# A mixer whose transposes are woven into its tiles, with the two S5 shuffles on the GpSimd queue

## The chip, the cores and the metric

The kernel runs on one core of a Trainium2 chip. The metric is the device time of one execution in microseconds (us). The kernel before takes 2861.14 us, the median of three runs (2859.89 to 2865.21).

## The reference, cut to what matters

The kernel computes one layer of a decoder trunk for 2048 tokens of width 1024: a norm, a token mixer, a residual, a norm, a mixture of experts, a residual, a final norm. The mixer's four branches read one projection of the normalised input (14 blocks of 128 columns):

```python
proj = xn @ w_in                      # (2048, 1024) @ (1024, 1792)
ya = short_conv_mixer(a_b, a_c, a_x, conv_a_w)
yb = pool_mixer(p_u, pool_w, pool_b, pool_scale)
yc = s5_mixer(s_u, ...)               # complex diagonal state space, gelu, then a gated linear unit
yd = rglru_mixer(l_x, l_g, ...)
ys = jnp.stack([ya, yb, yc, yd], axis=2)
branch = jnp.einsum('bskw,kwd->bskd', ys, branch_w)
gates = jax.nn.sigmoid(xn @ merge_gate_w + merge_gate_b).reshape(bn, s, N_BRANCH, d)
merged = jnp.sum(gates * branch, axis=2)
return merged @ w_out
```

## The kernel before, in words

**Stages.** `mix_branches` does the norm, the projection and the four branches, `merge_branches` the gates, the merge, the output projection, the residual, the second norm and the router's logits. `route`, the experts and the last sum follow, and nothing of them changes. Between stages all engines meet at a barrier. Every product in fp32 is made of three matmuls: an operand is split into a rounded high part and the low rest, and high·high, low·high and high·low are added in PSUM.

**The mixer's loop.** The tokens go in four chunks (c = 0 to 3) of 512. In a chunk, ScalarE squares and sums the rows (`squares`), VectorE makes the reciprocal root (`rms_scale`), ScalarE scales the rows (`scale_rows`, L456). TensorE then transposes them to feature-major in 8 steps of 4 transposes into two alternating PSUM banks (`turn_x`, L641); for each step ScalarE writes the high part (`x_highs`, L463) and VectorE the low part (`x_lows`, L793), and only then is the bank free again. 14 projection tiles follow (`tile`, L632), each 24 matmuls of 128x512, in the order of `F_ORDER`. Between the tiles stand the small products: `gates(c)` (L649), `states_in` (L663, reads `u4`), `states_out` (L674 and L676, the S5 output of the chunk), `pool_out` (L655) and `glu(c)` (L686, reads `yn`). Each tile's bank comes from one of two rings of two banks: `gr` is emptied by ScalarE, `dr` by VectorE; a ring's order of use is a list (`g_turns`, `d_turns`), so a bank that is late stops what stands behind it in TensorE's program.

**The weights.** In chunk 0 the 14 weight tiles come raw from DRAM (`load_raw`, four buffers), ScalarE makes the high part (L445), GpSimd the low part (L419), and SyncE spills both to DRAM (`spill`); three buffers hold them for TensorE. In the later chunks SyncE reloads them tile by tile (`load_win`, L313), two or three tiles ahead.

**The S5 shuffles.** The S5 branch needs its input with time folded onto the partitions. `turn_u(c)` stores `su` to DRAM (L328, 512 KB) and, once that has landed, loads `u4` in another shape (L333, 4 DMAs of 128 KB). `turn_y(c)` does the same with the branch's output: one store of `yg4` (L339) and 8 loads into `yn` (L344, 64 KB each), after which `glu(c)` can run. Both are in SyncE's own in-order program: where SyncE waits for a store to land, the weight reloads behind it wait too. In chunks 2 and 3 `turn_y(c-1)` stands after the reload of tile 3, behind the store of the transposed input `xT` (L322, 4 MB) and the load of the next chunk's rows (L317, 2 MB), and `turn_u(c)` after the reload of tile 5. `glu(c-1)` and then `states_in(c, ...)` stand between tiles 3 and 4 on TensorE.

**GpSimd** does the 14 low parts in chunk 0 and then the cosine and sine tables (L429 to L434), and nothing in the rest of the mixer.

**The merge.** `merge_branches` takes the tokens in four trips of 512. A trip reads the transposed input (as high and low part) and the four branches' outputs from DRAM, and for each of 8 output tiles and 4 branches k makes a gate product (8 accumulation steps) and a branch product (2 steps), three matmuls a step (L1377). Weights go through a ring of four raw buffers; ScalarE and VectorE split them (L1312, L1446). Before the first trip SyncE issues in this order: weights of k=0, `xT` high and low (4 DMAs, 4 MB), two pieces of the branches, weights of k=1 to 3, six small parameters (L1243), `w_out`.

## Time and profile before

| | us |
|---|---|
| median of 3 runs | 2861.14 |
| the profiled execution | 2863.44 |
| its span | 2861.8 |
| TensorE busy in it | 2445.9 (85%) |
| VectorE, ScalarE, GpSimd busy | 1446.1, 1035.9, 531.4 |

TensorE is the busiest engine. The page's row of 40 slices shows where it isn't busy (a digit is the busy share of 71.5 us in tenths): the first eight slices are the mixer, the ninth holds the start of the merge.

```
PE   5788697949999999999999999279999999998930
DVE  6578373624343343343433433846546564655648
PEclk 9889798979998999999999999589999999999975
```

The chain of the page's fourth part is followed back from the last instruction and ends within the last stage, so it says nothing about the mixer. For the mixer the table of windows, the waits of a stretch and the timeline are read instead.

### The profile page before, as it was taken

How to read it: one execution, taken by the hardware profiler on the slowest of the kernel's cores; microseconds unless marked ns; L12 is line 12 of the kernel's file. 1: busy time of each engine (PE TensorE's matmuls, PEld its weight loads, DVE VectorE, ACT ScalarE, POOL GpSimd, SP SyncE). 2: the span in 40 equal slices, each digit the busy share in tenths (PEclk: the TensorE clock that was granted, in tenths of full speed). 3: DMA queues.
4: the chain of work that ended last, by engine and by line, in shares of the span. 5: the costliest groups of instructions: out<-in, count | busy, mean ns of one | idle time of the engine just before them, and what ended most of it. 6: DMA issues, size and time to landing. Idle time of an engine off the chain costs nothing. (4 is left out here: it accounts for less than half of the span.)

```text
span 2861.8 us, 36672 instructions
## 1 busy us (share of the span) xinstructions
PE 2445.9 (85%) x11820; PEld 1877.7 (66%) x11821; DVE 1446.1 (51%) x2190; ACT 1035.9 (36%) x1254; POOL 531.4 (19%) x380
## 2 busy tenths in 40 slices
PE   5788697949999999999999999279999999998930
PEld 4566575638866887588758884167677676777730
DVE  6578373624343343343433433846546564655648
ACT  3424132212221222122212221146556565666621
POOL 2500000000000000000000000424433443354451
PEclk9889798979998999999999999589999999999975
DMA  8653655484462446344544444258677767778766
GB/s 250 219 210 118 211 179 177 147 261 143 138 205 89 137 127 203 107 120 144 167 143 120 135 132 166 95 221 319 240 267 286 279 261 263 290 296 322 289 260 280
DMA packets 394811, 573.81 MB, mean 201 GB/s; under 512 B 34960, under 2 KB 226704, under 8 KB 394768
## 3 DMA queue, kind: packets, MB, share of 16 engines
q1 hardware_dynamic: 361152, 475.47, 48.4%
q0 software_dynamic: 21680, 76.57, 7.1%
q10 hardware_dynamic: 11936, 21.24, 2.0%
q8 instruction: 21, 0.34, 0.0%
q14 instruction: 22, 0.18, 0.0%
HBM read 449.73 MB, written 123.47 MB: 200 GB/s over the span
## 5 line engine op out<-in xcount | busy, mean ns | idle before, releaser
L1377 PE MATMUL mrgps<-act_hi,w_hi 128*128 128x512 f32 x1280 | 504.4, 394 | 37.0 <-DMA act_lo<-xn_feature_major 21.0
L1377 PE MATMUL mrgps<-act_lo,w_hi 128*128 128x512 f32 x1280 | 502.7, 393 | 0.0
L1377 PE MATMUL mrgps<-act_hi,w_lo 128*128 128x512 f32 x1280 | 502.1, 392 | 0.0
L1733 POOL TENSOR_TENSOR w_lo<-w_raw,w_hi 128x1024 fp32r<-128x1024 f32 x128 | 326.9, 2588 | 241.4 <-ACT w_hi L1724 241.4
L1728 DVE TENSOR_TENSOR w_lo<-w_raw,w_hi 128x2048 fp32r<-128x2048 f32 x124 | 302.6, 2482 | 35.4 <-ACT w_hi L1719 35.4
L1377 PEld LDWEIGHTS mrgps<-act_hi,w_hi 128*128 128x128 f32 x1280 | 243.5, 190 | 90.2 <-DMA act_lo<-xn_feature_major 22.3
L1377 PEld LDWEIGHTS mrgps<-act_hi,w_lo 128*128 128x128 f32 x1280 | 243.2, 190 | 51.2
L1377 PEld LDWEIGHTS mrgps<-act_lo,w_hi 128*128 128x128 f32 x1280 | 243.6, 190 | 50.3
L1446 DVE TENSOR_TENSOR w_lo<-w_raw,w_hi 128x1280 fp32r<-128x1280 f32 x129 | 192.5, 1492 | 132.4 <-ACT w_hi L1312 130.7
L1329 ACT ACTIVATE gt<-mrgps,mb 128x512 f32<-128x512 f32 x128 | 88.4, 690 | 446.8 <-PE mrgps L1377 446.8
L1861 PE MATMUL exps<-w_hi,xT_hi 128*128 128x256 f32 (+1 forms) x768 | 247.5, 322 | 1.9 <-DVE xT_lo L2053 1.9
L1861 PE MATMUL exps<-w_lo,xT_hi 128*128 128x256 f32 (+1 forms) x768 | 245.6, 320 | 0.0
L1861 PE MATMUL exps<-w_hi,xT_lo 128*128 128x256 f32 (+1 forms) x768 | 245.6, 320 | 0.0
L1312 ACT ACTIVATE w_hi<-w_raw 128x1280 fp32r<-128x1280 f32 x129 | 164.5, 1275 | 210.1 <-DVE tmp L1467 135.3
L1719 ACT ACTIVATE w_hi<-w_raw 128x2048 fp32r<-128x2048 f32 x128 | 237.9, 1906 | 5.7 <-DMA w_raw<-in_expert_w_dram 5.7
L1293 POOL DMA_DIRECT2D expert_rows<-zeros x32 | 29.8, 932 | 1081.9 <-DVE w_lo L1446 1028.5
L1397 PE MATMUL mrgps<-wout,merged 128*128 128x512 f32 x512 | 222.1, 593 | 6.7 <-DVE merged L1469 6.7
L1467 DVE SCALAR_TENSOR_TENSOR tmp<-gt,mrgps 128x512 f32<-128x512 f32 x96 | 66.1, 688 | 301.2 <-PE mrgps L1377 301.2
L632 PE MATMUL mixps<-mix_xT_hi,win_hi 128*128 128x512 f32 x448 | 185.0, 413 | 36.5 <-DVEq L866 16.9
L632 PE MATMUL mixps<-mix_xT_lo,win_hi 128*128 128x512 f32 x448 | 182.1, 406 | 0.0
L632 PE MATMUL mixps<-mix_xT_hi,win_lo 128*128 128x512 f32 x448 | 181.3, 405 | 0.0
L1397 PEld LDWEIGHTS mrgps<-wout,merged 128*128 128x128 f32 x512 | 96.3, 190 | 125.1 <-issue 116.7
(377 smaller groups left out, 3649.3 us busy)
## 6 DMA issues: line engine op xcount, KB each, us to landing
w_raw<-in_expert_w_dram SPq DMA_DIRECT2D x128, 1024.0 KB, 8.9
w_raw<-in_merge_gate_w_dram SPq DMA_DIRECT2D x132, 512.0 KB, 4.1
w_raw<-in_expert_w_dram SPq DMA_DIRECT2D x32, 2048.0 KB, 14.2
expert_rows<-zeros POOLq DMA_DIRECT2D x32, 1008.0 KB, 7.2
win_hi<-w_in_parts SPq DMA_DIRECT2D x42, 512.0 KB, 3.5
win_lo<-w_in_parts SPq DMA_DIRECT2D x42, 512.0 KB, 5.3
w_raw<-in_branch_w_dram SPq DMA_DIRECT2D x132, 128.0 KB, 3.9
expert_rows<-ysb ACTq DMA_DIRECT2D x64, 256.0 KB, 3.1
```

The costliest lines, as they stand in the source:

```text
L632: last = pe.matmul(bank[:], w[:, n % NW, cols], x[:, k], start=(k + j == 0), stop=(k == KD - 1 and j == 2))
L1293: pool.dma_start(dram["y"][ds(i * FILL, FILL), :].rearrange("(p r) (q n) -> p (r q) n", r=2, n=256), zeros[:].unsqueeze(1).to_broadcast([F ...
L1312: act.activation(w_hi[:, k % 2].rearrange("p k n -> p (k n)"), w_raw[:, k].rearrange("p k n -> p (k n)"), ACT.Copy).then_inc(w_hi_set, 1)
L1329: act.activation(gt[:], gbank[k % 2][:], ACT.Tanh, scale=0.5, bias=mb[:, k, ds(d, 1)]).then_inc(g_free, 1)
L1377: last = pe.matmul(bank[:], w[:, k % 2, kk], x[:, a], start=(kk == w_tiles[0] and x is act_hi and w is w_hi), stop=(kk == w_tiles[-1] and ...
L1397: last = pe.matmul(bbank[h][:], merged[:, kk, t * P:(t + 1) * P], wout[:, kk, h * 512:(h + 1) * 512], start=(kk == 0), stop=(kk == KD - 1))
L1446: dve.tensor_tensor(lo, w_raw[:, k].rearrange("p k n -> p (k n)"), hi.bitcast(F32), ALU.subtract).then_inc(w_split, 1)
L1467: dve.scalar_tensor_tensor(tmp[:], gt[:], 1.0, bbank[k % 2][:], ALU.add, ALU.mult).then_inc(b_free, 1)
L1719: act.activation(self.hi13[:, i], self.raw13[:, i], ACT.Copy).then_inc(self.high13, 1)
L1728: eng.tensor_tensor(self.lo13[:, i], self.raw13[:, i], self.hi13[:, i].bitcast(F32), ALU.subtract).then_inc(self.split13, 1)
L1733: eng.tensor_tensor(self.lo2[:, f], self.raw2[:, f], self.hi2[:, f].bitcast(F32), ALU.subtract).then_inc(self.split2, 1)
L1861: last = pe.matmul(bank[:, 0:n], x[:, k], weights[:, 2 * w + k // 4, cols], start=(k + i == 0), stop=(k == KD - 1 and i == 2))
```

## The change

1. `turn_u` and `turn_y` are issued by GpSimd. `turn_u(0)` stands after its eighth weight split, all others after the tables, in the order u(1), y(0), u(2), y(1), u(3), y(2), y(3). SyncE's program no longer holds a wait for them. The large transfers of a chunk stand after the reload of tile 4 (in chunk 0 after the spills of tiles 7 and 9, where they were after that of tile 1).
2. `first_tiles(c)` weaves the transposes with tiles 0 and 1.
3. The small products move: `gates(0)` before tile 8, `states_out(c-1)` ahead of all transposes, `glu(c-1)` behind tile 7 (that of chunk 0 behind tile 13 of chunk 1), `states_out(3)` behind tile 8 of chunk 3 in two banks of their own. ScalarE's and VectorE's parts of the S5 output are cut up between the eight steps of `x_highs` and `x_lows`.
4. The raw merge weights are loaded during chunk 3 into a buffer which they share with `xin`. `x_hi` and `x_lo` of chunk 3 stay in SBUF, and the merge takes chunk 3 first (the trips go 3, 0, 1, 2), so its start loads neither. Its pieces are issued first, then the parameters.

```diff
+    LAG = 4
-                return f(*range(10)) + gates(0) + f(10, 11)
+                return f(*range(8)) + gates(0) + f(8, 9, 10, 11)
-            return f(0, 1, 2, 3) + glu(c - 1) + f(4, 5) + gates(c) + f(*range(6, 12)) + (glu(c) if c == CH - 1 else [])
+            return f(*range(6)) + gates(c) + f(6, 7) + glu(c - 1) + f(8, 9, 10, 11) + (glu(c) if c == CH - 1 else [])
@@ SyncE
-                if i == 1:
-                    store_xT(0)
+                if i == 7:
                     sp.wait_ge(t_full, KD)
                     load_x(1)
-                if i == 3:
-                    turn_u(0)
+                if i == 9:
+                    store_xT(0)
             for c in range(1, CH):
                 for i in range(NF):
                     load_win(c, i)
-                    if i == 3:
+                    if i == 4:
                         store_xT(c)
                         if c + 1 < CH:
                             load_x(c + 1)
-                        if c > 1:
-                            turn_y(c - 1)
-                    if i == (10 if c == 1 else 5):
-                        turn_u(c)
+                    if i == 8 and c == CH - 1:
+                        sp.wait_ge(t_full, KD * CH)
+                        for k in range(NBR):
+                            load_merge_weights(sp, io, w_raw, merge_w_in, k, 0)
+                    if i == 12 and c > 1:
+                        store(2, c - 1, glu_done, yn)
-            turn_y(CH - 1)
@@ GpSimd
             for i in range(NF):
                 pool.wait_ge(w_high, i + 1)
                 pool.tensor_tensor(w_lo[:, i % NW], raw[i % NR], ...).then_inc(w_split, 1)
+                if i == 7:
+                    turn_u(pool, 0)
...
+            for c in range(1, CH):
+                turn_u(pool, c)
+                turn_y(pool, c - 1)
+            turn_y(pool, CH - 1)
@@ ScalarE, chunks 2 and 3
+                x_highs(c, (0, 1))
                 y_square(c - 1, 0)
+                x_highs(c, (2,))
+                y_square(c - 1, 1)
+                x_highs(c, (3,))
                 y_tanh(c - 1, 0)
-                x_highs(c)
-                y_square(c - 1, 1)
+                x_highs(c, (4,))
                 y_tanh(c - 1, 1)
-                for i in range(4):
-                    evac(c, i)
-                glu_tanh(c - 1)
-                for i in (4, 5):
+                x_highs(c, (5, 6, 7))
+                for i in range(6):
                     evac(c, i)
                 lru_gates(c)
                 gate_tanh(c)
                 for i in (6, 7):
                     evac(c, i)
                 lru_root(c)
+                glu_tanh(c - 1)
@@ TensorE
+            def first_tiles(c):
                 pe.wait_ge(xh_full, c * Q + Q)
+                turn_x(c, 0)
+                turn_x(c, 1)
+                open_tile(c, 0)
                 for k in range(KD):
+                    pe.wait_ge(x_split, c * KD + k + 1)
+                    tile_part(c, 0, k)
+                    if k + 2 < KD:
+                        turn_x(c, k + 2)
+                    if k == LAG:
+                        open_tile(c, 1)
+                    if k >= LAG:
+                        tile_part(c, 1, k - LAG)
+                for k in range(KD - LAG, KD):
+                    tile_part(c, 1, k)
@@ VectorE, chunk 2 (chunk 3 has y_poly and y_gelu of its own between glu_out and pool_result)
+                    pool_mix(c)
+                    lru_out(c)
+                    pool_result(c)
+                    glu_out(c - 1)
                     rms_scale(s, c + 1)
@@ merge, SyncE
-            load_weights(0, 0)
-            load_x_parts(0, 0)
-            load_x_parts(0, 1)
             for c in range(PIECES):
-                load_piece(0, c)
-            for k in range(1, NBR):
-                load_weights(k, 0)
+                load_piece(TRIPS - 1, c)
+                sp.sem_inc(xp_in[c], 32)
```

In what follows the engines' programs are given in order, a row for each instruction or run of like ones. SyncE's program in chunk 2 before, from the store of the transposed input (it stands between the reloads of tiles 3 and 4; `late` is the buffer of `yg4` and `yn`):

```order
L322 DMA xn_feature_major<-mix_xT_hi 128x8x512 [waits xT_split]
L322 DMA xn_feature_major<-mix_xT_lo 128x8x512
L317 DMA xin<-in_x_dram 128x1024 x4
L339 DMA s_outputs<-late 128x1024 [waits yn_in,y_gelu]
L344 DMA late<-s_outputs 32x4x128 [waits ys_out2,y_out]
L344 DMA late<-s_outputs 32x4x128 x7
L313 DMA win_hi<-w_in_parts 128x1024 [waits act_tile_full,win_out1]
L313 DMA win_lo<-w_in_parts 128x1024
L328 DMA s_inputs<-su 128x2x512 [waits u4_in,act_tile_free]
L333 DMA u<-s_inputs 32x8x128 [waits dve_tile_full,u_out]
L333 DMA u<-s_inputs 32x8x128 x3
L349 DMA branches<-lg 128x2x512 [waits yd_full]
```

The same place now:

```order
L362 DMA xn_feature_major<-xn_hi 128x8x512 [waits xT_split]
L362 DMA xn_feature_major<-xn_lo 128x8x512
L357 DMA w_raw<-in_x_dram 128x1024 x4
L353 DMA win_hi<-w_in_parts 128x1024 [waits act_tile_full,win_out2]
L353 DMA win_lo<-w_in_parts 128x1024
L366 DMA branches<-lg 128x2x512 [waits yd_full]
L353 DMA win_hi<-w_in_parts 128x1024 [waits act_tile_full,win_out0]
L353 DMA win_lo<-w_in_parts 128x1024
```

And GpSimd's program for u(2) and y(1), where it had nothing:

```order
L312 DMA s_inputs<-su 128x2x512 [waits u4_in,act_tile_free]
L317 DMA u<-s_inputs 32x8x128 [waits dve_tile_full,u_out]
L317 DMA u<-s_inputs 32x8x128 x3
L323 DMA s_outputs<-late 128x1024 [waits yn_in,y_gelu]
L328 DMA late<-s_outputs 32x4x128 [waits ys_out2,y_out]
L328 DMA late<-s_outputs 32x4x128 x7
```

The waits for landed stores have left SyncE, and u now precedes y.

TensorE's program at the start of chunk 2 before, from the last rows of `states_out(1, 0)`; two more steps are shown of eight, all ahead of the first projection matmul:

```order
L674 MATMUL mixps<-u,toeplitz 128x128
L676 MATMUL mixps<-late,DE 128x128 x2
L641 MATMUL mixps<-ident,xin 128x128 [waits xT_split,xhat_full]
L641 MATMUL mixps<-ident,xin 128x128 x3
L641 MATMUL mixps<-ident,xin 128x128 [waits xT_split]
L641 MATMUL mixps<-ident,xin 128x128 x3
```

The same place now, behind both `states_out` (`w_raw` is the buffer that holds `xin` and the identity):

```order
L728 MATMUL mixps<-u,toeplitz 128x128
L730 MATMUL mixps<-late,DE 128x128 x2
L675 MATMUL mixps<-w_raw 128x128 [waits xT_split,xhat_full]
L675 MATMUL mixps<-w_raw 128x128 x3
L675 MATMUL mixps<-w_raw 128x128 [waits xT_split]
L675 MATMUL mixps<-w_raw 128x128 x3
L662 MATMUL mixps<-xn_hi,win_hi 128x512 [waits xT_split,act_tile_free,win_in1]
L662 MATMUL mixps<-xn_lo,win_hi 128x512
L662 MATMUL mixps<-xn_hi,win_lo 128x512
L675 MATMUL mixps<-w_raw 128x128 [waits xT_split]
L675 MATMUL mixps<-w_raw 128x128 x3
```

Three projection matmuls now stand behind each step of four transposes.

SyncE's program from the start of the merge before (14 DMAs ahead of the parameters, 4 MB of them `xn_feature_major`):

```order
L1230 DMA w_raw<-in_merge_gate_w_dram 128x8x128
L1232 DMA w_raw<-in_branch_w_dram 128x2x128
L1227 DMA act_hi<-xn_feature_major 128x4x512
L1227 DMA act_lo<-xn_feature_major 128x4x512
L1227 DMA act_hi<-xn_feature_major 128x4x512
L1227 DMA act_lo<-xn_feature_major 128x4x512
L1222 DMA act_raw<-branches 128x4x512 x2
```

And now:

```order
L1275 DMA act_raw<-branches 128x4x512 x2
L1286 DMA mb<-in_merge_gate_b_dram 128x32x1
L1286 DMA g<-in_norm_g_dram 128x1024
L1286 DMA rw<-in_router_group_w_dram 128x8x4
L1286 DMA rw<-in_router_expert_w_dram 128x8x32
```

Two pieces are all that stands ahead of the parameters.

## Rows read from the trace of the kernel before

**Rows 1.** Windows by stage: start:end, length, busy us (x count) by engine, clock, DMA.

```profile
core 0: us, PE busy (x) PEld busy (x) DVE busy (x) ACT busy (x) POOL busy (x), PEclk, DMA share, GB/s
0.00:147.00 147.00, 99.76 (x384) 76.50 (x385) 88.53 (x234) 56.39 (x77) 61.83 (x67) 0.93 0.71 234
147.00:312.00 165.00, 134.23 (x722) 107.68 (x723) 126.73 (x242) 54.77 (x82) 0.00 (x0) 0.88 0.44 160
312.00:447.00 135.00, 108.73 (x473) 83.72 (x472) 70.84 (x127) 39.15 (x56) 0.00 (x0) 0.90 0.55 187
447.00:580.00 133.00, 106.38 (x447) 80.77 (x445) 66.51 (x111) 27.94 (x40) 0.00 (x0) 0.92 0.51 174
580.00:622.00 42.00, 12.70 (x30) 8.93 (x30) 7.70 (x6) 6.94 (x5) 1.94 (x4) 0.62 0.97 293
```

**Rows 2.** Timeline of SyncE's queue, chunk 2: start, us, queue, line, tiles, count.

```profile
329.81 1.08 SPq L339 DMA_DIRECT2D s_outputs<-late  x1
...
347.60 0.37 SPq L328 DMA_DIRECT2D s_inputs<-su  x1
355.15 1.80 SPq L333 DMA_DIRECT2D u<-s_inputs  x4
```

**Rows 3.** Timeline of PE, tile 3 to tile 4 in chunks 2 and 3 [idle before].

```profile
346.89 6.61 PE L686 MATMUL mixps<-late,glw 128*128 128x512 f32 x8 [12.15 <-DMA late<-s_outputs]
...
359.56 3.69 PE L663 MATMUL mixps<-u,BT 128*128 128x128 f32 x16 [6.07 <-DMA u<-s_inputs]
...
475.63 5.39 PE L686 MATMUL mixps<-late,glw 128*128 128x512 f32 x8 [6.08 <-DMA late<-s_outputs]
488.24 3.78 PE L663 MATMUL mixps<-u,BT 128*128 128x128 f32 x16 [7.21 <-DMA u<-s_inputs]
491.67 0.77 PE L632 MATMUL mixps<-mix_xT_hi,win_hi 128*128 128x512 f32 x1
```

**Rows 4.** Timeline of PE, the transposes of each chunk and what follows.

```profile
22.66 1.94 PE L641 MATMUL mixps<-ident,xin 128*128 128x128 f32 x8 [22.66 <-ACT xin L456]
...
34.45 0.76 PE L632 MATMUL mixps<-mix_xT_hi,win_hi 128*128 128x512 f32 x1 [1.66 <-DVE mix_xT_lo L793]
...
149.41 0.77 PE L641 MATMUL mixps<-ident,xin 128*128 128x128 f32 x5 [2.71 <-ACT xin L456]
...
292.37 1.04 PE L641 MATMUL mixps<-ident,xin 128*128 128x128 f32 x8
...
431.76 1.03 PE L641 MATMUL mixps<-ident,xin 128*128 128x128 f32 x8
```

**Rows 5.** Timeline of PE in chunk 2, first matmuls six tiles apart.

```profile
382.22 0.47 PE L632 MATMUL mixps<-mix_xT_hi,win_hi 128*128 128x512 f32 x1 [1.75 <-ACT lru L500]
...
415.77 1.02 PE L655 MATMUL mixps<-pooled,bd 128*128 128x512 f32 x2
```

**Rows 6.** Timeline of POOL and PE in chunk 0, tile 5.

```profile
67.76 2.36 POOL L419 TENSOR_TENSOR win_lo<-late,win_hi 128x1024 fp32r<-128x1024 f32 x1 [15.88 <-ACT win_hi L445]
70.17 0.80 PE L632 MATMUL mixps<-mix_xT_hi,win_hi 128*128 128x512 f32 x1 [5.63 <-POOL win_lo L419]
```

**Rows 7.** Timeline of ACT, the scaled rows of chunk 1, then of chunk 3.

```profile
145.09 4.27 ACT L456 ACTIVATE xin<-xin,rst 128x1024 f32<-128x1024 f32 x4 [8.42 <-DVEq L786]
...
423.85 2.19 ACT L456 ACTIVATE xin<-xin,rst 128x1024 f32<-128x1024 f32 x2 [3.07 <-DVEq L786]
```

**Rows 8.** Timeline of PE and ACT, the start of the merge.

```profile
590.26 0.80 PE L1377 MATMUL mrgps<-act_hi,w_hi 128*128 128x512 f32 x1 [17.78 <-DMA act_lo<-xn_feature_major]
601.49 1.91 ACT L1305 ACTIVATE act_hi<-act_raw 128x2048 fp32r<-128x2048 f32 x1 [15.32 <-DMA act_raw<-branches]
619.26 1.27 ACT L1312 ACTIVATE w_hi<-w_raw 128x1280 fp32r<-128x1280 f32 x1 [13.10 <-DVE mb L1452]
622.18 0.79 PE L1377 MATMUL mrgps<-act_hi,w_hi 128*128 128x512 f32 x1 [13.47 <-DVE w_lo L1446]
```

**Rows 9.** The page's fifth part, the only large DMAs that GpSimd issues.

```profile
L1293 POOL DMA_DIRECT2D expert_rows<-zeros x32 | 29.8, 932 | 1081.9 <-DVE w_lo L1446 1028.5 <-issue 53.4
```

More of the change, by code:

```diff
@@ L42 @@
 NSTEP = (T - P) // HB
+WK = KD + 2
 NB = 94
@@ L166, in mix_branches @@
         sre, sim_ = ps[3], ps[4]
+        last_y = Turns(sem("last_y_full"), sem("last_y_free"), ps[3:5], [("y", CH - 1, u) for u in range(2)])
         tb = ps[6:8]
@@ L633, in tile, with tile_part @@
-                last.then_inc(ring.full, 1)
-            def turn_x(c):
+                (dr if f in (4, 5) else gr).open(pe, ("f", c, f))
+            def tile_part(c, i, k):
+                n = c * NF + i
+                f = F_ORDER[i]
+                ring, key = dr if f in (4, 5) else gr, ("f", c, f)
+                cols = slice(k * P, (k + 1) * P)
+                for j, (w, x) in enumerate(((w_hi, x_hi), (w_hi, x_lo), (w_lo, x_hi))):
+                    last = pe.matmul(ring.bank(key)[:], w[:, n % NW, cols], x[:, k], start=(k + j == 0), stop=(k == KD - 1 and j == 2))
+                if k == KD - 1:
+                    last.then_inc(ring.full, 1)
@@ L636, in turn_x, with tile @@
+            def tile(c, i):
+                open_tile(c, i)
+                for k in range(KD):
+                    tile_part(c, i, k)
+            def turn_x(c, k):
+                if c * KD + k >= 2:
+                    pe.wait_ge(x_split, c * KD + k - 1)
+                for t in range(Q):
+                    last = pe.transpose(tb[k % 2][:, t * P:(t + 1) * P], xin[:, t, k * P:(k + 1) * P], ident[:])
+                last.then_inc(t_full, 1)
+            def first_tiles(c):
                 pe.wait_ge(xh_full, c * Q + Q)
+                turn_x(c, 0)
+                turn_x(c, 1)
+                open_tile(c, 0)
@@ L689, in _ @@
             pe.wait_ge(consts, 3)
-            turn_x(0)
-            for i in range(10):
+            first_tiles(0)
+            for i in range(2, 8):
                 tile(0, i)
+            pe.wait_ge(par_in, 16 * len(params))
+            pe.wait_ge(bd_in, 16 * 12)
+            gates(0)
+            tile(0, 8)
+            tile(0, 9)
             pe.wait_ge(masks_set, 1)
@@ L743, in _ @@
             pool_out(1)
-            glu(0)
             tile(1, 12)
             tile(1, 13)
-            states_out(1, 0)
-            turn_x(2)
-            states_out(1, 1)
+            glu(0)
             for c in range(2, CH):
-                for i in range(4):
-                    tile(c, i)
-                glu(c - 1)
+                states_out(c - 1, 0)
+                states_out(c - 1, 1)
+                first_tiles(c)
+                tile(c, 2)
+                tile(c, 3)
                 states_in(c, 0)
@@ L1281, in _ @@
                 sp.wait_ge(w_in[k], 32 * (1 + TRIPS * KD))
+            for c in range(2):
+                sp.wait_ge(xp_in[c], 32 * (1 + TRIPS))
         @block.gpsimd
```

275 lines of the change are left out of this document (135 added, 140 removed).

## The prediction

> **What bounds the kernel now.** I read the page's row of slices first: after the ninth slice TensorE is at 9 tenths for most of the way, and nothing of those stages changes, so the change can only act where the digits are low, in the mixer and at the start of the merge. The table of windows [rows 1] sizes that: TensorE is idle for 147 − 99.8 = 47.2 us in chunk 0, 30.8 in chunk 1, 26.3 and 26.6 in chunks 2 and 3, and 29.3 in the first 42 us of the merge, 160.2 us in all. That is the ceiling of any gain that doesn't remove matmuls (this change removes none). The timelines then say who ends each wait. In chunks 2 and 3 it is the S5 shuffles [rows 3]: 12.15 and 6.08 us for y, 6.07 and 7.21 us for u. Tile 3 ends at 346.89 − 12.15 = 334.74 in chunk 2 and tile 4 starts at 359.56 + 3.43 = 363.0 (states_in takes 488.24 to 491.67 in chunk 3): 28.3 us, of which 6.6 are glu and 3.4 states_in. The queue shows why: SyncE issues the store of y at 329.81, holds everything behind it till it has landed and the loads are issued, stores u at 347.60 and loads it only at 355.15 [rows 2]. So y's shuffle takes 17 us, to 346.89, and u stands behind it. At each chunk's start transposes run at the pace of the copies: 22.66 to 34.45 for 32 of them that need 4 × 1.94 = 7.8 us [rows 4]. In the merge the first product waits until 590.26 for 4 MB of transposed input, the pieces of the branches come 11 us later, and the weights of k=1 are split only after the parameters have landed (619.26) [rows 8].
>
> **The change part by part.** The sum is made at places that TensorE passes: for each, its time before and the time I expect.
>
> *Chunk 0, to the first transposes of chunk 1 (149.41 [rows 4]).* Weaving puts tiles 0 and 1 into the gaps of the transposes. Before, the two end 11.8 + 2 × 5.6 = 23.0 us after 22.66 (a tile costs 5.59 us: six in 33.55 [rows 5], plus a start at lower clock); now TensorE's own work, 32 transposes and two tiles, is 7.8 + 11.2 = 19.0, and only the first step's copies are not covered by it: −4 to −6, and my schedule, in which some transposes run faster than 1.94 for eight, takes −6. Tile 5 waits 5.63 us because ScalarE's split of its raw weights, and GpSimd behind it (15.88 us idle), wait for a load that stands behind 6 MB [rows 6]; with these 6 MB moved behind tiles 7 and 9 this wait goes: −5.6. `gates(0)` now comes before tile 8 and waits for its block-diagonal weights, which VectorE prepares, some 3 us, that were nothing before. turn_u(0) on GpSimd costs five DMAs at 0.93 us [rows 9] and the time its store takes to land (7.6 us, 347.60 to 355.15 [rows 2]), about 12 us in which no low part is made; GpSimd is ahead of TensorE by a tile or two there, which hides most. The end of the chunk is a chain: last tile of the gated recurrence, gates, output, sum of squares, reciprocal root, scaled rows. It starts sooner by what TensorE gained and by the two tiles 10 and 11 no longer following all else: I get 136.5, −13. The bounds: −4 (only the weave) and −20.
>
> *Chunk 1, to the first transposes of chunk 2 (292.37).* The weave gives −5 again, so tile 1 of chunk 1 ends some 18 us sooner. But behind tile 11 stands now a longer chain: glu(0) has moved behind tile 13, ScalarE does its tanh and then the squares of chunk 2, VectorE its reciprocal root, then conv_a, and the y products, which now all stand ahead of the first transpose. My schedule of it gives 291.5: nearly all is given back, −1. Bounds −13 (the chain is as short as before) and +5.
>
> *Chunk 2, to tile 4 (363.0).* Two states_out were split by the transposes before; from the first transpose to the end of tile 1 I take 19.5 us (7.8 + 11.2 + a start), where before it was 31.2 (292.37 to tile 3's end at 334.74, less two tiles of 5.6): −12. Then tiles 2 and 3 end at 322.4. glu(1) is gone from here (6.6), its wait too (12.15), and u waits only for its own shuffle: the store goes once ScalarE has emptied the second half of the input, about 312, the loads 7.5 us later (347.60 to 355.15 before [rows 2]), and they land 4.4 us after that (355.15 to 359.56), 324, or 325 with what GpSimd's own issue adds. With the 3.4 us of states_in behind it tile 4 starts at 328.4: −34.6. *To chunk 3's transposes (431.76):* glu(1) comes back behind tile 7 with 5.4 us of matmuls [rows 3] and a wait of about 3.4 (its two banks wait for ScalarE's tanh behind the square root), and the y products stand ahead of the transposes: 405.5, −26.
>
> *Chunk 3.* Weave −7; tile 4 at 442.4 against 491.67: −49 (the waits of 6.08 and 7.21 and the glu, less a wait of 2 for u). glu(2) returns behind tile 7, states_out(3) comes between tiles 8 and 9, and y(3) is shuffled beside tiles 9 to 13, so glu(3) needs little waiting: the mixer's last store at −50. Bounds for this and the last part together: ±10, since y(3) needs nine DMAs of GpSimd and a landed store, some 8 + 8 + 4 = 20 us, against about 22 us of tiles.
>
> *Merge start.* Before, from the mixer's last product (590.26 − 17.78 = 572.48) to k=1 (622.18) it takes 49.7 us [rows 8], 42.0 of them after the barrier at 580.2. Now input and weights are there, so k=0 begins some 3 us after the barrier; the two pieces (2 MB instead of 6.6 MB ahead) land after 5 to 6.5, are split by two ScalarE copies of 1.91 and VectorE's rests until 11.6; the parameters land by 11; then the weights of k=1 (1.27 and 1.5): k=1 at 14.7 after the barrier. 42.0 − 14.7 = −27. Bounds −10 (the parameters land as late after the pieces as now, 17.8 us from 601.49 to 619.26 [rows 8]) and −32 (all at the rate of the split).
>
> *Nothing elsewhere.* The trips' order is a register; the merge weights of k=0 to 3 (2.6 MB) load beside tiles 8 to 13 of chunk 3, where DMA is at 0.51 of its time [rows 1].
>
> The sum, against the profiled execution's 2863.44 (1.6 above its span, 2.3 above the median, within the spread of the runs): −50 −27 = −77, 2786; against the median 2784. I say 2787, because small waits that a plan doesn't see only add.
>
> **A rule against it.** The 32 DMAs that GpSimd issues in the merge took 0.93 us each [rows 9]. The Trainium skill (SBUF — State Buffer, section "SBUF: two separate sides") says that GpSimd writes the descriptors of its DMAs itself, that these stand still while VectorE holds the port pair they share, and advises SyncE's or ScalarE's queue. What this case shows of such a sharing: the norm's scaled rows wait 8.42 us for VectorE in chunk 1, while GpSimd computes its tables, and 3.07 us in chunk 3, when it rests [rows 7]. In chunks 2 and 3 VectorE is busy for half the time [rows 1], so such meetings are likely. Were each DMA lengthened as the norm was (8.42/3.07 = 2.7 times, 2.5 us), u's five would take 8 us more, and y's nine 14.
>
> **The rivals.**
> A. GpSimd's DMAs are 2.5 us each. u, which my schedule already has no cover for, is 8 us later in chunks 2 and 3, y(3) 14 less its 2 of slack: 2787 + 28 = 2815. For it: rows 7. Against it: rows 9. 15%.
> B. Chunk 0 gains nothing beyond the weave: the loads of raw weights, already at 71% of DMA time [rows 1], or GpSimd's pause for u(0) set the pace there: +13 to +16, 2803. 12%.
> C. The merge's start saves only the 4 MB: parameters in small packets still land last, −10 in place of −27: 2804. 8%.
> D. It goes better: the chain of chunk 1 to 2 keeps the 13 us it starts sooner, −12, and TensorE's clock in chunk 1 is 0.93 as in chunk 0 and not 0.88 [rows 1], 134.2 × 0.05 = −7: 2768. 10%.
> E. The other side: a DMA that GpSimd issues from and to such tiles costs it many times what the stores of zeroes cost [rows 9]. On the path lie u's five in chunks 2 and 3, and y(3)'s nine with 2 us of slack: 19 DMAs. To lose 77 us each must take (77 + 2)/19 = 4.2 us more than 0.93, so it decides from 5.1 us on; at 8 us each the time is 2787 + 19 × 7.1 − 2 = 2920. For it: nothing in the trace of before has GpSimd store or load 32 or 128 partitions directly. 4%.
> That the moves don't do what they say I hold for excluded by the order of the programs.
>
> **How the numbers follow.** Forecast 51%, its own range 2776 to 2799; A 15, B 12, C 8, D 10, E 4. From 2766 to 2820 lie the forecast, A, B, C and half of D, some 85% before errors of a kind I don't foresee. Faster by over 0.2% (5.7 us, about what a measurement of this kernel tells from no change): all but E and a sum of mishaps, 0.95; within 0.2%, 0.02; slower 0.03.
>
> **What would show it.** In the windows of the changed profile: TensorE's first transposes near 136, 291 and 405; no wait on `late` or `u` above 3 us except glu(3)'s; GpSimd's DMAs near 1 us; k=1 of the merge 15 us after its barrier. I am wrong if the transposes of chunk 1 start after 145 (B), if TensorE waits for `u` over 6 us (A), or if transposes of chunk 2 start before 285 (D).

## The result, and the profile after

| | before | after |
|---|---|---|
| median of 4 runs each (us) | 2862.71 (2859.89 to 2865.21) | 2834.21 (2833.71 to 2837.61) |
| ratio, 95% interval | | 0.9904 (0.9889 to 0.9920) |
| span of the profiled execution | 2861.8 | 2832.1 |

28.5 us faster, where 76 were forecast. The page's row of slices (TensorE's busy share in tenths) looks much as before, the mixer's eight slices included:

```profile
PE   6678698879999999999999999189999999998930
```

The windows of the changed kernel (columns as in [rows 1]), cut where TensorE starts the transposes of chunks 1, 2 and 3 (152, 308, 437), at the end of the mixer (570) and where the merge reaches k=1 (592):

```profile
0.00:152.00 152.00, 94.14 (x384) 72.29 (x385) 107.28 (x244) 58.88 (x79) 64.78 (x72) 0.89 0.70 233
152.00:308.00 156.00, 125.26 (x693) 101.28 (x694) 109.92 (x218) 46.02 (x70) 8.03 (x14) 0.90 0.40 138
308.00:437.00 129.00, 105.52 (x470) 83.07 (x468) 72.90 (x132) 38.87 (x56) 8.08 (x14) 0.92 0.62 224
437.00:570.00 133.00, 107.26 (x478) 83.17 (x476) 73.39 (x122) 33.98 (x51) 12.86 (x23) 0.94 0.59 194
570.00:592.00 22.00, 8.98 (x31) 7.01 (x31) 7.94 (x6) 6.84 (x5) 1.72 (x4) 0.73 0.87 259
```

TensorE is still idle for 57.9, 30.7, 23.5, 25.7 and 13.0 us, 151 in all; before it was 160 up to the same place [rows 1]. So only a third of what is gained here is idle time. Up to k=1 of the merge TensorE is busy for 441.1 us where it was 461.8, with the same matmuls: the 128 transposes are busy for 22.6 us where they were 28.4, the 32 products of glu for 14.4 where they were 19.2, and the granted clock over the stretch is 0.90 where it was 0.88. VectorE is busy for 107 of the first 152 us, 19 us more than in the first 147 before, though it ran only ten instructions more. The longest waits stand in TensorE's timeline (in brackets how long it was idle before the instruction, and for whom):

```profile
90.65 6.15 PE L701 MATMUL mixps<-xc,bd 128*128 128x512 f32 x8 [15.43 <-DVE xc L851]
...
149.11 2.05 PE L707 MATMUL mixps<-pooled,bd 128*128 128x512 f32 x2 [12.97 <-DVE va L923]
152.07 1.97 PE L675 MATMUL mixps<-w_raw 128*128 128x128 f32 x8 [0.92 <-ACT w_raw L475]
...
274.52 0.77 PE L662 MATMUL mixps<-xn_hi,win_hi 128*128 128x512 f32 x1 [9.50 <-DVEq L916]
300.89 0.80 PE L728 MATMUL mixps<-u,toeplitz 128*128 128x128 f32 x2 [9.21 <-DVE va L923]
307.96 1.04 PE L675 MATMUL mixps<-w_raw 128*128 128x128 f32 x8
317.97 0.79 PE L662 MATMUL mixps<-xn_hi,win_hi 128*128 128x512 f32 x1 [8.97 <-DMA win_lo<-w_in_parts]
353.49 3.78 PE L715 MATMUL mixps<-u,BT 128*128 128x128 f32 x16 [8.12 <-DMA u<-s_inputs]
437.03 1.04 PE L675 MATMUL mixps<-w_raw 128*128 128x128 f32 x8
473.46 3.78 PE L715 MATMUL mixps<-u,BT 128*128 128x128 f32 x16 [7.82 <-DMA u<-s_inputs]
545.87 0.48 PE L662 MATMUL mixps<-xn_hi,win_hi 128*128 128x512 f32 x1 [3.40 <-DVEq L916]
573.00 0.79 PE L1424 MATMUL mrgps<-xn_hi,w_hi 128*128 128x512 f32 x1 [10.94 <-DVE w_lo L1493]
591.94 0.79 PE L1424 MATMUL mrgps<-xn_hi,w_hi 128*128 128x512 f32 x1 [10.01 <-DVE w_lo L1493]
```

The 12.97 us before the transposes of chunk 1 are the end of the chain through the gated recurrence: VectorE frees the bank (`va`) only when the reciprocal root behind that chain is done, and ScalarE scales the rows at the same time. No wait for `late` (y) is left, of 18.2 us [rows 3]. Against the plan's marks:

| place on TensorE | before | forecast | after | missed in the stage that ends here |
|---|---|---|---|---|
| transposes of chunk 1 | 149.4 | 136.5 | 152.1 | +15.6 |
| transposes of chunk 2 | 292.4 | 291.5 | 308.0 | +0.9 |
| transposes of chunk 3 | 431.8 | 405.5 | 437.0 | +15.1 |
| mixer's last product ends | 572.5 | 522.5 | 562.1 | +8.0 |
| k=1 of the merge | 622.2 | 545.2 | 591.9 | +7.2 |

The last column sums to 46.8 us, which is nearly all of what is missing (2834.2 less the forecast 2787 is 47.2). Of the 30.2 us gained at k=1, 19.8 are the merge's start (49.7 us from the mixer's last product before, 29.9 now) and 10.4 the mixer.

### The profile page after: what moved, and what is told of

It is laid out like the page before. It is cut to its first block and busy times, and to the rows that moved or that the text cites. A ratio compares the mean times of both kernels' runs of the same rounds, so it can differ in the third digit from the quotient of the medians.

```text
span 2832.1 us, 36678 instructions
## 1 busy us (share of the span) xinstructions
PE 2423.3 (86%) x11820; PEld 1866.0 (66%) x11821; DVE 1457.3 (51%) x2190; ACT 1034.9 (37%) x1254; POOL 563.8 (20%) x436
## 5 line engine op out<-in xcount | busy, mean ns | idle before, releaser
L1424 PE MATMUL mrgps<-xn_hi,w_hi 128*128 128x512 f32 x1024 | 403.2, 394 | 20.9 <-DVE w_lo L1493 20.9
L1424 PE MATMUL mrgps<-xn_lo,w_hi 128*128 128x512 f32 x1024 | 402.2, 393 | 0.0
L1424 PE MATMUL mrgps<-xn_hi,w_lo 128*128 128x512 f32 x1024 | 401.7, 392 | 0.0
L1776 DVE TENSOR_TENSOR w_lo<-w_raw,w_hi 128x2048 fp32r<-128x2048 f32 x124 | 303.3, 2487 | 34.6 <-ACT w_hi L1767 34.6
L1424 PEld LDWEIGHTS mrgps<-xn_hi,w_hi 128*128 128x128 f32 x1024 | 194.9, 190 | 63.1 <-issue 22.2
L1424 PEld LDWEIGHTS mrgps<-xn_lo,w_hi 128*128 128x128 f32 x1024 | 194.7, 190 | 40.4
L1424 PEld LDWEIGHTS mrgps<-xn_hi,w_lo 128*128 128x128 f32 x1024 | 194.5, 190 | 40.6
L662 PE MATMUL mixps<-xn_hi,win_hi 128*128 128x512 f32 x448 | 185.7, 414 | 40.2 <-DVEq L916 12.9
L662 PE MATMUL mixps<-xn_lo,win_hi 128*128 128x512 f32 x448 | 179.3, 400 | 0.0
L662 PE MATMUL mixps<-xn_hi,win_lo 128*128 128x512 f32 x448 | 178.9, 399 | 0.0
## 6 DMA issues: line engine op xcount, KB each, us to landing
w_raw<-in_expert_w_dram SPq DMA_DIRECT2D x32, 2048.0 KB, 14.4
```

Of the source, the lines that this page charges most:

```text
L662: last = pe.matmul(ring.bank(key)[:], w[:, n % NW, cols], x[:, k], start=(k + j == 0), stop=(k == KD - 1 and j == 2))
L1424: last = pe.matmul(bank[:], w[:, k % 2, kk], x, start=(kk == w_tiles[0] and j == 0), stop=(kk == w_tiles[-1] and j == 2))
L1776: eng.tensor_tensor(self.lo13[:, i], self.raw13[:, i], self.hi13[:, i].bitcast(F32), ALU.subtract).then_inc(self.split13, 1)
```

## The experiments

Each ran in three rounds beside the kernel before, and its ratio is to that. The difference given last is of medians, to the changed kernel's 2834.2. The changed kernel was not run again beside them, and the kernel before had a median of 2862.7 with it and of 2863.7 to 2865.8 with the experiments, so each difference is uncertain by some 3 us beyond the noise; by the ratios every edit gains 1 to 5 us more, or loses 1 to 5 us less, than the differences say. The interval of every ratio is about ±0.0017, ±5 us. The places on TensorE come from one profile each and are sharper than the totals: where two kernels run the same program they agree within 1 us.

### One wait of SyncE's (e1_store)

```diff
-                if c == 1:
-                    store(2, 0, glu_done, yn)
+                    if i == 2 and c == 2:
+                        store(2, 0, glu_done, yn)
```

> The changed kernel with one store moved: the S5 branch's output of chunk 0 (yn, waits for glu_out(0)) is issued after the reload of the third tile of chunk 2, and no longer before the reload of the first. Theory (SyncE's in-order wait for glu_out holds the reload): TensorE's wait of 8.97 us for win_lo at the first tile of chunk 2 goes, the reload is issued when tile 11 of chunk 1 has ended, and as nothing else of chunk 2 hangs on it the whole is about 8 us shorter, 2826. Rival (the reload was late for DMA traffic or the chain of VectorE and ScalarE sets the start anyway): the wait turns into one for VectorE's low parts of the same size, 2834.

2825.0, ratio 0.9856 (0.9839 to 0.9872), −9.2. The same places as above:

```profile
307.24 1.03 PE L675 MATMUL mixps<-w_raw 128*128 128x128 f32 x8
311.12 0.47 PE L662 MATMUL mixps<-xn_hi,win_hi 128*128 128x512 f32 x1 [2.85 <-DVE xn_lo L843]
345.54 3.79 PE L715 MATMUL mixps<-u,BT 128*128 128x128 f32 x16 [8.14 <-DMA u<-s_inputs]
```

(The first row is the first transpose of chunk 2, the second the first matmul of its tile 0.) The wait of 8.97 is gone, 2.85 for VectorE take its place, and the product with `u` comes 8.0 us sooner. The theory holds. In SyncE's timeline of the changed kernel one sees it directly: the store that waits for glu_out(0) goes at 310.88 and the reload behind it at 311.37, though the buffer had been free since tile 11 of chunk 1, which ended at 263:

```profile
310.88 0.39 SPq L366 DMA_DIRECT2D branches<-late  x1
311.37 0.41 SPq L353 DMA_DIRECT2D win_hi<-w_in_parts  x1
```

### Six megabytes beside the shuffle (e2_big)

```diff
-                    if i == 4:
+                    if i == (4 if c == 1 else 7):
                         store_xT(c)
```

> The changed kernel with the 4 MB store of the transposed input and the 2 MB load of the next rows behind the reload of tile 7 and not of tile 4 in chunks 2 and 3. Theory (the u shuffle is late because the 6 MB are issued in the same microsecond as its store): TensorE's waits of 8.1 and 7.8 us for u fall to 2 to 3 us each, the landing of u's store falls from 8 to 3 us, the whole is some 10 us shorter, 2824. Rival (GpSimd's DMAs land late by themselves: u's loads took 9.3 us from issue to the product): the waits stay above 6 us, 2834.

(Chunk 3 loads no further rows, so there it is 4 MB that move.) 2821.8, ratio 0.9845 (0.9829 to 0.9861), −12.4. The waits for `u` are 4.61 and 4.36 where they were 8.12 and 7.82, so the theory holds for nearly half of each. GpSimd's timeline in chunk 2, first of the changed kernel, then of this one:

```profile
335.50 0.72 POOL L312 DMA_DIRECT2D s_inputs<-su  x1 [76.64 <-ACT su L513]
344.20 2.34 POOL L317 DMA_DIRECT2D u<-s_inputs  x4 [7.98 <-DMA s_inputs<-su]
346.53 0.70 POOL L323 DMA_DIRECT2D s_outputs<-late  x1
```

```profile
333.90 0.72 POOL L312 DMA_DIRECT2D s_inputs<-su  x1 [76.16 <-ACT su L513]
339.86 2.34 POOL L317 DMA_DIRECT2D u<-s_inputs  x4 [5.24 <-DMA s_inputs<-su]
342.19 0.58 POOL L323 DMA_DIRECT2D s_outputs<-late  x1
```

The store lands after 5.2 us and no longer 8.0. The loads still land 6.5 us (median) after their issue, against 2.9 when SyncE issues them (next run). That seems to speak for the rival, but GpSimd as the issuer is not enough for it. In chunk 1 of the changed kernel GpSimd issues the same four loads, and they land after 2.8 us; VectorE is busy for 3.3 of the 3.4 us around them and the DMA engines for 0.51 of the time. In chunks 2 and 3 they land after 6.9 and 7.0 us with the DMA engines at 1.05, here after 6.5 and 6.4 at 0.96 and 1.00, and SyncE's 2.8 to 2.9 were at 0.63 to 0.74. No run holds the traffic fixed and changes the issuer, so this rest stays open.

### The shuffles back on SyncE (e3_sp)

```diff
+                    if c == 1 and i == 10:
+                        turn_u(sp, 1)
+                    if c == 1 and i == 12:
+                        turn_y(sp, 0)
+                    if c > 1 and i == 4:
+                        turn_u(sp, c)
+                        turn_y(sp, c - 1)
...
-                if i == 7:
-                    turn_u(pool, 0)
```

> The changed kernel with all shuffles back on SyncE: u(0) after spill 3, u(1) and y(0) after the reloads of tiles 10 and 12 of chunk 1 as before the change, in chunks 2 and 3 u(c) and then y(c-1) after the reload of tile 4, ahead of the 6 MB; y(3) at the end. If moving them to GpSimd is what gained: slower than the changed kernel by 10 us or more, with TensorE waiting for weight tiles 7 and 8 behind SyncE's waits for landed stores. If it gained nothing (u is late for the traffic, y has time in the new order anyway): u's wait falls to 3 us since its transfers are ahead of the 6 MB and land alone, chunk 0 gains some us on VectorE and GpSimd, y(3) is as early; the whole is 2822 to 2834. I hold the second for likelier.

2848.5, ratio 0.9939 (0.9922 to 0.9955), +14.3. I had held the other outcome for likelier. The waits for `u` are down to 0.60 and 0.66 us, but in each chunk a weight tile behind it is now waited for:

```profile
372.25 0.80 PE L666 MATMUL mixps<-xn_hi,win_hi 128*128 128x512 f32 x1 [18.10 <-DMA win_lo<-w_in_parts]
...
497.46 0.80 PE L666 MATMUL mixps<-xn_hi,win_hi 128*128 128x512 f32 x1 [13.66 <-DMA win_lo<-w_in_parts]
```

These weight reloads stand in SyncE's program behind two waits for landed stores and the 6 MB (4 in chunk 3). Against this placement on SyncE, the only one tried, moving the shuffles is worth 14 us in the new order (10 by the ratios). In the new order GpSimd's pause for u(0) costs chunk 0 little: without it `gates(0)` starts at 89.62 against 90.65.

### That part alone (e7_bpool)

The kernel before, with SyncE's calls of `turn_u` and `turn_y` taken out and GpSimd's put in, u(0) after its sixth low part:

```diff
+            turn_u(pool, 1)
+            turn_y(pool, 0)
+            for c in range(2, CH):
+                turn_y(pool, c - 1)
+                turn_u(pool, c)
+            turn_y(pool, CH - 1)
```

> The kernel before with one part of the change alone: GpSimd issues the shuffles (u(0) after its sixth low part, u(1), y(0), then y(c-1) and u(c) after the tables) and SyncE's program only loses them. Everything else, the places of glu, the weave, the merge, is as before. If the queue was what held the shuffles: y(1) is stored some 5 us after its gelu and glu(1) starts 10 us sooner, u is loaded before glu ends, TensorE's waits for them in chunks 2 and 3 fall from 31.5 to 10 us: 20 us faster, 2845. If traffic and GpSimd's later landing hold them: 0 to 8 us faster. The last shuffle y(3) was at the end already and may be 2 us later.

2848.8 beside 2863.7, ratio 0.9947 (0.9931 to 0.9964), −15 us to the kernel before: between the two theories. In chunks 2 and 3 TensorE waits no longer for y, and for u 8.34 and 8.05 us. The places show more than the total. The transposes of chunk 1 start at 155.09 where they started at 149.41, since in this order GpSimd's pause for u(0) does cost: the low part behind it is waited for.

```profile
83.37 0.80 PE L631 MATMUL mixps<-mix_xT_hi,win_hi 128*128 128x512 f32 x1 [6.12 <-POOL win_lo L410]
```

The transposes of chunk 2 start 6.7 us later than before (299.05 against 292.37) and the mixer's last product ends 13.9 sooner (558.62 against 572.48), so in chunks 2 and 3 the part gains 20.5 us, what the first theory said, and chunk 0 gives 6 back. With e3_sp it splits the whole about in half: this part alone −15, everything but this part −14 (−17 to the runs beside it), both −28.5.

### VectorE's order in chunk 0 (e4_conv)

`lru_conv(0)` with the three bias halvings goes ahead of the second half of the S5 parameter work.

```diff
+            dve.wait_ge(par_in, 16 * len(params))
+            for i in (BA, BX, GB):
+                s.mark(dve.tensor_scalar(vec[:, i, :], ...))
+            lru_conv(0)
             s.link(dve.tensor_scalar(pt(T1), pt(X), -88.0, 1.0 / 128, ALU.max, ALU.mult))
```

> The changed kernel with VectorE's lru_conv(0) (and the halving of three bias vectors that stood before it) moved ahead of the second half of the S5 parameter work in chunk 0. Theory (gates(0) stands now before tile 8 and waits 15.4 us for xc, which is last in VectorE's parameter work): the wait falls to under 3 us, tiles 8 to 13 end 12 us sooner; the recurrence's chain starts sooner by 12 and the transposes of chunk 1 at about 141 against 152: 2823. Rival (the parameter work itself, needed for the states of chunk 1, or the tables set the time): PE's wait moves to a later place in chunk 1, 2832.

2819.7, ratio 0.9839 (0.9822 to 0.9855), −14.6.

```profile
120.77 2.04 PE L707 MATMUL mixps<-pooled,bd 128*128 128x512 f32 x2 [5.59 <-DVE va L923]
131.64 2.04 PE L707 MATMUL mixps<-pooled,bd 128*128 128x512 f32 x2 [8.83 <-DVE va L923]
134.60 1.97 PE L675 MATMUL mixps<-w_raw 128*128 128x128 f32 x8 [0.92 <-ACT w_raw L475]
```

The wait of 15.43 is gone and chunk 1's transposes start at 134.6, 17.5 us sooner (the forecast of the whole change had said 136.5). At the merge's k=1 10.8 of these are left (581.16 against 591.94).

### What makes VectorE late there (e10_pieces)

The changed kernel's VectorE (parameter work, 0.17 us an instruction) and GpSimd at one place:

```profile
46.74 2.32 DVE L1015 TENSOR_SCALAR bgcg<-bgcg 128x8 f32<-128x8 f32 x1
49.09 0.17 DVE L1016 TENSOR_SCALAR bgcg<-bgcg 128x8 f32<-128x8 f32 x1
```

```profile
46.63 2.40 POOL L432 TENSOR_TENSOR win_lo<-late,win_hi 128x1024 fp32r<-128x1024 f32 x1 [2.20 <-ACT win_hi L464]
```

An instruction that takes 0.17 us elsewhere takes 2.32 here and ends just after GpSimd's subtraction does. Between its start and the convolution VectorE's parameter work takes 49.3 us (38.23 to 87.48) and took 37.1 (34.60 to 71.71) before, when GpSimd waited for weights from 51.9 to 67.8 [rows 6]. In the longer stretch GpSimd makes nine subtractions and in the shorter one four: five more of 2.40 us are 12.0 of the 12.2 us. Three of the nine come in a row behind the pause for u(0), and there a single instruction is held until the third is done:

```profile
73.30 8.03 DVE L1083 TENSOR_SCALAR vec<-vec 128x2 f32<-128x2 f32 x3
```

```profile
74.18 6.98 POOL L432 TENSOR_TENSOR win_lo<-late,win_hi 128x1024 fp32r<-128x1024 f32 x3
```

The experiment cuts each subtraction in four.

```diff
-                pool.tensor_tensor(w_lo[:, i % NW], raw[i % NR], ...)
+                for h in range(4):
+                    cs = slice(256 * h, 256 * (h + 1))
+                    pool.tensor_tensor(w_lo[:, i % NW, cs], raw[i % NR][:, cs], ...)
```

> The changed kernel with each of GpSimd's 14 low parts (128x1024, 2.40 us) cut into four instructions of 128x256. Theory (VectorE's small instructions, 0.17 us alone, stand still for as long as a subtraction of GpSimd runs: 2.3 us several times between 38 and 83 us, and that is what makes xc late): with pieces of 0.6 us VectorE gets in between, each blocked instruction takes at most 0.7 us, and the parameter work ends up to 8 us sooner; gates(0) at 83 to 88 us against 90.65, the whole up to 8 us faster. Rival (VectorE loses GpSimd's busy time however it is cut, or its long instructions have another cause): gates(0) within 1.5 us of 90.65 and instructions of 2.3 us still there.

2832.0, ratio 0.9892 (0.9876 to 0.9909), −2.3: no difference. The held instructions are shorter, as the theory said, and there are more of them, as the rival said:

```profile
48.38 0.65 DVE L1035 TENSOR_SCALAR bgcg<-bgcg 128x8 f32<-128x8 f32 x1
49.06 0.65 DVE L1039 TENSOR_TENSOR bgcg<-bgcg 128x8 f32<-128x8 f32 x1
49.75 0.66 DVE L1040 TENSOR_TENSOR bgcg<-bgcg 128x8 f32<-128x8 f32 x1
50.44 0.65 DVE L1041 TENSOR_SCALAR bgcg<-bgcg 128x8 f32<-128x8 f32 x1
```

The stretch of parameter work takes 48.7 us where it took 49.3, again beside nine subtractions' worth of pieces, and behind the pause VectorE doesn't get in between the pieces either (four instructions in 9.68 us at 73.50). `gates(0)` starts 66.9 us after the first transpose (86.59 after 19.73), in the changed kernel 68.0. VectorE loses GpSimd's busy time however it is cut. That nine subtractions meet it here and four before is counted, not varied: no run changes their number alone. The Trainium skill (SBUF — State Buffer, section "Who interferes with whom") calls the pair of ports that the two share an exclusive lock, held for a whole instruction. These rows agree: VectorE is held for 2.3 us by a subtraction of 2.4 and for 0.65 by a quarter of one.

### The chain from chunk 1 to chunk 2 (e6_sq)

```diff
-            glu_tanh(0)
             for c in range(2, CH):
                 act.wait_ge(yd_full, 2 * c)
                 squares(c)
                 scale_rows(c)
+                if c == 2:
+                    glu_tanh(0)
```

> The changed kernel with ScalarE's squares and row scaling of chunk 2 ahead of glu_tanh(0) and not behind it. Theory (the start of chunk 2 hangs on squares, root, conv_a in one row behind the last product of chunk 1, so the 15 us that chunk 1 had been ahead in the plan are of no use): VectorE's root is done before 280, conv_a frees its banks by 292, TensorE's wait of 9.2 us for va goes, the transposes of chunk 2 start at 299 to 301 against 308. The reload of the first tile is then late by the same amount (it waits behind glu_out(0) on SyncE), so that wait of 9 us grows by up to what was gained: the whole gains 0 to 7 us, 2827 to 2834, and only with the store moved as well would the full 15 show.

2817.7, ratio 0.9841 (0.9824 to 0.9857), −16.6, more than expected.

```profile
295.24 1.03 PE L676 MATMUL mixps<-w_raw 128*128 128x128 f32 x8
300.32 0.79 PE L663 MATMUL mixps<-xn_hi,win_hi 128*128 128x512 f32 x1 [4.05 <-DMA win_lo<-w_in_parts]
```

The transposes of chunk 2 start at 295.2 against 308.0, the wait of 9.21 for `va` is gone, and the reload's wait shrank to 4.05 where I had expected it to grow. In the changed kernel VectorE had been idle for 21.2 us before the root (up to 296.59), because ScalarE's squares stood behind the tanh of glu(0), which waits for TensorE's last product of chunk 1.

### The merge's start (e5_mb)

```diff
+            sp.dma_start(mb[:], ...).then_inc(mb_in, 16)
             for c in range(PIECES):
                 load_piece(TRIPS - 1, c)
...
-            dve.wait_ge(par_in, 16 * len(params))
+            dve.wait_ge(mb_in, 16)
             dve.tensor_scalar(mb[:], mb[:], 0.5, None, ALU.mult).then_inc(half_b, 1)
```

> The changed kernel with the gate bias (mb, 16 KB) issued first at the start of the merge, ahead of the two pieces, with a semaphore of its own, so that VectorE's halving of it waits no longer for the norm gains and the router's parameters behind it. Theory (the split of the weights of k=1 stands behind that halving, which waits for the last of six parameters, 18.5 us after the barrier): k=1 starts some 6 us sooner, 16 us after the barrier where it was 22; 0.2% of the whole, 2828. Rival (the output weights and parameters keep the queues and k=1 or the pieces are late instead): within 2 us of the changed kernel.

2834.1, ratio 0.9896 (0.9879 to 0.9912), −0.1: the theory failed as tried. ScalarE's two copies of the pieces, in this run:

```profile
579.82 1.91 ACT L1353 ACTIVATE ys_hi<-act_raw 128x2048 fp32r<-128x2048 f32 x1 [7.62 <-DMA act_raw<-branches]
585.26 1.91 ACT L1353 ACTIVATE ys_hi<-act_raw 128x2048 fp32r<-128x2048 f32 x1 [3.52 <-DMA act_raw<-branches]
```

In the changed kernel they start at 575.01 and 578.04, with SyncE's first DMA at 569.7 (570.8 here). With the 16 KB of gate bias in front, the 2 MB behind it came 4 to 6 us later. Issued behind the pieces, as in the run of all five edits below, the edit works: k=1 comes 16.5 us after SyncE's first DMA where it came after 22.2.

### The weave (e8_unweave)

```diff
-                turn_x(c, 0)
-                turn_x(c, 1)
...
+                for k in range(KD):
+                    turn_x(c, k)
+                pe.wait_ge(x_split, (c + 1) * KD)
+                tile(c, 0)
+                tile(c, 1)
```

> The changed kernel with all 8 steps of transposes ahead of tiles 0 and 1 again in every chunk, the rest unchanged. Theory (the weave gains 5 to 7 us a chunk where nothing else ends later): chunk 0 shows the loss of 6 us at tile 1 but gates(0) waits for VectorE in any case, so nothing is lost there; chunk 1 loses 5 at tile 1, chunks 2 and 3 lose 5 each: slower than the changed kernel by 10 to 16 us, 2845 to 2850. Rival (the weave only shifts waiting to the weight tiles): under 4 us.

2840.8, ratio 0.9922 (0.9906 to 0.9939), +6.6, less than expected; the two intervals overlap, and it is the places that show the loss. In chunk 0 taking the weave out even gains: the wait for `xc` is 6.41 and not 15.43, and chunk 1's transposes start at 148.46, 3.6 us sooner. By chunk 2's this is gone again (308.25 against 307.96). Chunk 2 loses nothing (351.63 against 353.49 at the product with `u`, behind the late reload), and chunk 3 loses 7.1 us up to that product (480.55 against 473.46). The weave worked in four chunks and was worth something in one.

### The waits taken together (e9_all, e11_allunw)

The edits of e1, e2, e4 and e6, and e5's with the gate bias issued behind the pieces:

```diff
             for c in range(PIECES):
                 load_piece(TRIPS - 1, c)
                 sp.sem_inc(xp_in[c], 32)
+            sp.dma_start(mb[:], ...).then_inc(mb_in, 16)
+            for dst, src in params[1:]:
```

> The changed kernel with five edits at once: the store of yn of chunk 0 behind three reloads, the 6 MB behind the reload of tile 7, lru_conv(0) ahead of half the parameter work, ScalarE's squares and scaling of chunk 2 ahead of glu_tanh(0), and the gate bias with a semaphore of its own, issued right behind the two pieces of the merge. If the shortfall of the forecast was these waits and each is by itself: the gains of the runs with one edit each (-9, -12, -15, -18 us by their medians less the changed kernel's) add to -54, less what two of them share at the start of chunk 2 (5 us), with 3 to 5 us more at the merge: 2782 to 2790, about what was forecast for the change. If they hide each other (the same waits seen from several places): 2800 to 2815.

2783.6 (2783.1 to 2784.4) beside 2865.0, ratio 0.9718 (0.9702 to 0.9734): −81 us to the kernel before, −50.6 to the changed one. This lies in the first theory's range: the single edits' differences (−9.2, −12.4, −14.6, −16.6 and, with the bias ahead of the pieces, −0.1; the expectation has −18 for e6_sq) sum to −53, so each wait was there by itself.

```profile
134.40 1.97 PE L676 MATMUL mixps<-w_raw 128*128 128x128 f32 x8 [0.91 <-ACT w_raw L475]
...
282.58 1.03 PE L676 MATMUL mixps<-w_raw 128*128 128x128 f32 x8
315.68 3.78 PE L716 MATMUL mixps<-u,BT 128*128 128x128 f32 x16 [4.48 <-DMA u<-s_inputs]
...
396.43 1.04 PE L676 MATMUL mixps<-w_raw 128*128 128x128 f32 x8
...
541.90 0.49 PE L1427 MATMUL mrgps<-xn_hi,w_hi 128*128 128x512 f32 x1 [4.52 <-DVE w_lo L1496]
```

k=1 comes at 541.9, where the plan had 545.2. Two of the five edits are in places that no term of the plan covered (e1, e2), two in terms that it had too small (e4, e5), and one undoes a chain that it had seen and accepted (e6). Of the 80.3 us gained at k=1 53.6 are idle time; the other 26.7 are busy time, with the granted clock of the stretch at 0.94. And with the weave taken out of this kernel, by e8's edit:

> The kernel with the five edits (2783.6 us), with all 8 steps of transposes ahead of tiles 0 and 1 again. In the changed kernel the weave was worth 6.6 us of the 25 forecast, since VectorE's parameter work, the recurrence's chain and a late reload stood behind it in chunks 0, 1 and 2. With the first and the last of these moved out of the way it should be worth 5 to 7 us in three of four chunks: 2798 to 2804. If it stays near 7 us (2791), the chains behind it, and not the reload, are what makes it worthless.

2800.6, ratio 0.9778 (0.9762 to 0.9794), 17.0 slower, as expected in all, but not spread as expected: chunks 0 and 1 lose 1.9 and 1.2 us by the starts of the next transposes (136.29 and 285.70), chunk 2 7.0 (406.58) and chunk 3 8.2. The weave is worth 17 us here and 6.6 in the changed kernel.

## Why the prediction was wrong

The parts of the change did what the plan said, and TensorE's own durations were good: from the first transpose to the end of tile 1 it took 17.7 us in chunk 3, where the plan had 19.5 for chunk 2. The plan failed in what stood behind or beside them, each time in the same direction, and most of all in chunk 0.

- *Chunk 0, "136.5, −13"*: +15.6. The step that failed is that `gates(0)` "waits for its block-diagonal weights, which VectorE prepares, some 3 us": the wait is 15.4, and for `xc`. The weave starts VectorE's parameter work 3.6 us later, and with GpSimd no longer short of weights nine of its subtractions and not four fall into that work and hold VectorE for 12 us more. Lifting a wait from GpSimd put it on VectorE. e4_conv shows the place; e10_pieces shows the hold; that the lifted wait brought the five more is read from the two traces. The gates came 10.7 us sooner than before (90.65 against 101.36) but two more tiles stand between them and ScalarE's tanh and root that follow (121.14, before 119.97), so the chain ended where it had.
- *Chunk 1, "−1"*: right in its length (155.9 us against 155.0). The plan took the longer chain behind tile 11 as given; e6_sq shows that it wasn't needed, since with squares and scaling ahead of the tanh chunk 2's transposes start 12.7 us sooner.
- *Chunk 2, "−34.6" at tile 4*: the reload behind the store of yn (8.97, e1_store) was in no term. Of u's own shuffle 13 us were planned from the issue of its store ("about 312") to the product (325), with a wait of 2.6 behind tile 3; measured are 18.0 (335.50 to 353.49) and 8.12. The store took 8.7 us to land for the 7.5 of [rows 2], and the loads 9.3 for 4.4, or 5.4 with GpSimd's own issue. Both were taken from SyncE's queue of before, and the 6 MB that start with u's store were forgotten; they are nearly half of the wait (e2_big), and what makes the rest is open.
- *Chunk 3*: the same for u (7.82 where 2 were planned), which is 5.8 of the 8.0 us missed up to the mixer's last product; the rest isn't traced. The 3.40 at tile 12 is no part of it, TensorE waited 3.56 there before. y(3) was right: TensorE doesn't wait for it.
- *Merge, "the parameters land by 11"*: they land at 18.5 after SyncE's first DMA (588.18), and k=1 comes at 22.2 and not 14.7. SyncE's queue is held for 7.6 us at the second DMA behind the pieces, the norm's gains:

```profile
571.27 7.63 SPq L1286 DMA_DIRECT2D g<-in_norm_g_dram  x1
```

It isn't these gains that cost it. In e5_mb their issue takes 0.45 us, and the same hold meets a router parameter issued later:

```profile
574.57 0.45 SPq L1288 DMA_DIRECT2D g<-in_norm_g_dram  x1
575.76 7.58 SPq L1288 DMA_DIRECT2D rw<-in_router_expert_w_dram  x1
```

What sets the moment of the hold no run shows.

- *The ceiling* of 160.2 us of idle time was none. Of the 30.2 us gained at k=1 only 9.6 are idle time; 20.7 came off TensorE's busy time, which the prediction took as fixed.
- *The rivals.* A said that u is 8 us late, for the price of GpSimd's DMAs; u is late, but the DMAs cost GpSimd 0.58 to 0.72 us each with VectorE half busy, so its mechanism is refuted, and E's with it. B's +13 to +16 came, by another cause than its two. C came by 7 of its 17 us. I gave each its own chance and its own time and let none meet another; together and in part they make 2834, above the range's 2820. D's first half (the chain from chunk 1 to 2 could be short) is what e6_sq found, but only by an edit. The chances from 2766 to 2820 add to 91 (51, 15, 12, 8 and half of 10) and not to the 85 given, so the confidence was higher still than it reads.

## What to carry to other kernels

A plan of what each engine does next has to carry every wait in a queue's order, not only those the change speaks of: here one store, one tanh and one convolution in an unlucky place each ate 9 to 17 us that had been won elsewhere. When an engine that can hold another up loses its wait, count its busy time on the other one too. Idle time is no ceiling for a gain where the granted clock moves, as it did here (0.88, 0.90 and 0.94 up to k=1). And when a part seems worthless (the weave, 6.6 us), test it again once the waits behind it are gone (17.0).

## What the runs showed of the hardware

- VectorE's instructions of 0.17 us last 2.27 to 2.40 us when they meet a GpSimd subtraction of 2.40, and 0.62 to 0.73 when it is cut in four. Behind three subtractions in a row VectorE gets through three small instructions in 8.03 us. What VectorE loses in all stays the same (49.3 us of parameter work, and 48.7 with the pieces).
- GpSimd issues a DMA from or to 32 or 128 partitions in 0.54 to 0.92 us, the loads of u(1) in 0.58 with VectorE busy nearly all the time. These landed after 2.8 us (median) with the DMA engines busy for 0.51 of the time; those of u(2) and u(3) after 6.9 and 7.0 at 1.05, in e2_big after 6.5 and 6.4 at 0.96 and 1.00. SyncE's of the same shape landed after 2.8 to 2.9 at 0.63 to 0.74.
- With a 16 KB DMA of single numbers (the gate bias) issued ahead of two of 1 MB, these landed 4 to 6 us later.
- SyncE's queue is held for 7.6 us at one DMA behind the pieces of the merge: the norm's gains in the changed kernel, a router parameter in e5_mb, where the gains take 0.45 us.
